# Out-projection products of the first token half moved from the sample sequences into the prompt attention, with the page gathers cut in two

## What is computed

```python
attn = nsa_attention(q, q_pos0, kv_cmp, kv_slc, kv_win, win_pos0, gates, w_cmp_k, w_cmp_v)
conv_out, conv_state = short_conv(xin, bg, cg, conv_prev, conv_w)
mix = jnp.einsum('bte,ed->btd', jnp.concatenate([attn, conv_out], axis=-1), w_out)
h = layer_norm(ALPHA * x + mix, ln1_g, ln1_b)
```

## Time and profile before

| | |
|---|---|
| Median of 3 runs | 2712.2 us |
| Profiled execution, its own time | 2708.6 us |
| Its span in the trace | 2706.8 us |
| PE busy | 2593.7 us, 96% |
| DVE, ACT, POOL busy | 74%, 40%, 3% |
| Granted TensorE clock, mean | 0.986 of full speed |
| DMA | 480.20 MB, 177 GB/s |
| Prompt attention | about 641 to 796 us |
| Sample sequences | about 796 to 1077 us |

### The profile page before, as it was taken

The page is one execution under the profiler, slowest core; times in us unless marked ns, Lnnn a source line. Parts: engine busy times, 40 slices in busy tenths (PEclk is TensorE's granted clock), DMA queues, the critical chain, the costliest instruction groups (busy, mean ns, idle before and its releaser), DMA issues.

```text
span 2706.8 us, 51737 instructions
## 1 busy us (share of the span) xinstructions
PE 2593.7 (96%) x20061; PEld 2477.8 (92%) x20061; DVE 2004.7 (74%) x3181; ACT 1073.2 (40%) x1361; POOL 70.3 (3%) x118
## 2 busy tenths in 40 slices
PE   8999999998889999987999999999999999999998
PEld 8999999995657777887999999999999999999997
DVE  5788732326875555689888888888888888888898
ACT  3111111115874444455555555555433333333333
POOL 1000000000000100000000000000000000000001
PEclk9999999998999999998999999999999999999998
DMA  8776643316026775754555555555795556555642
GB/s 260 231 240 207 191 85 79 79 49 237 2 71 213 246 247 176 213 158 138 187 185 187 190 189 188 185 185 185 277 313 181 185 177 211 184 182 180 194 126 86
DMA packets 514888, 480.20 MB, mean 177 GB/s; under 512 B 49276, under 2 KB 465300, under 8 KB 503862
## 3 DMA queue, kind: packets, MB, share of 16 engines
q1 hardware_dynamic: 509722, 411.57, 48.7%
q0 software_dynamic: 4736, 67.18, 6.6%
q10 hardware_dynamic: 332, 0.11, 0.0%
HBM read 387.89 MB, written 99.16 MB: 180 GB/s over the span
## 4 chain that ended last, share of the span: by engine, by line
PE 64%; DVE 6%; ACT 3%; issue 2%; DMA 1%; SPq 1%; DVEq 0%; ACTq 0%
PE ps L2619 50%; PE ps L2535 3%; PE ps L2462 3%; PE ps L2440 2%; PE ps L2330 1%; PE ps L2400 1%; PE ps L2384 1%; PE ps L2320 1%; DVE pS L1574 1%; PE ps L2344 1%; DMA f_b<-f_scratch 1%; PE ps L2416 1%; DVE w_sl L1774 0%; ACT sS L1000 0%; ACT pT L962 0%
## 5 line engine op out<-in xcount | busy, mean ns | idle before, releaser
L1128 ACT ACTIVATE w_sh<-w_s 128x1024 fp32r<-128x1024 f32 (+1 forms) x512 | 473.6, 949 | 783.3 <-PE ps L2619 522.6
L2619 PE MATMUL ps<-f_b,w_sh 128*128 128x288 f32 x3584 | 713.8, 295 | 8.4 <-DMA f_b<-f_scratch 6.0
L1774 DVE TENSOR_TENSOR w_sl<-w_s,w_sh 128x1024 fp32r<-128x1024 f32 (+1 forms) x512 | 554.3, 1088 | 123.9 <-ACT w_sh L1128 123.5
L2619 PEld LDWEIGHTS ps<-f_b,w_sh 128*128 128x128 f32 x3584 | 574.3, 189 | 11.0 <-DMA f_b<-f_scratch 7.0
L2619 PE MATMUL ps<-f_b,w_sl 128*128 128x288 f32 x1792 | 527.1, 294 | 0.0
L2619 PE MATMUL ps<-h_u,w_sh 128*128 128x288 f32 x2560 | 514.3, 296 | 11.4 <-DVE h_u L1909 10.9
L2619 PEld LDWEIGHTS ps<-h_u,w_sh 128*128 128x128 f32 x2560 | 411.1, 189 | 12.9 <-issue 6.8
L2619 PE MATMUL ps<-h_u,w_sl 128*128 128x288 f32 x1280 | 376.6, 294 | 0.0
L2619 PEld LDWEIGHTS ps<-f_b,w_sl 128*128 128x128 f32 x1792 | 338.9, 189 | 0.0
L861 ACT ACTIVATE w_hi<-w_raw 128x2048 fp32r<-128x2048 f32 x61 | 116.9, 1916 | 484.9 <-PE ps L2171 466.3
L2171 PE MATMUL ps<-x_hi,w_hi 128*128 128x288 f32 x1408 | 302.7, 297 | 0.0
(11 more groups left out here) (322 smaller groups left out, 3340.3 us busy)
## 6 DMA issues: line engine op xcount, KB each, us to landing
w_s<-in_w_mlp SPq DMA_DIRECT2D x512, 256.0 KB, 3.7
f_scratch<-f_st SPq DMA_DIRECT2D x32, 2016.0 KB, 9.0
f_b<-f_scratch SPq DMA_DIRECT2D x56, 1152.0 KB, 8.0
w_raw<-in_w_in SPq DMA_DIRECT2D x90, 512.0 KB, 5.1
e_raw<-in_w_out SPq DMA_DIRECT2D x16, 512.0 KB, 4.3
e_raw<-in_w_out SPq DMA_DIRECT2D x64, 128.0 KB, 3.3
wb<-in_cache_win SPq DMA_DIRECT2D x8, 1024.0 KB
w_raw<-in_w_out SPq DMA_DIRECT2D x64, 128.0 KB, 2.9
```

Of the source, the lines that this page charges most:

```text
L1128: nc.scalar.activation(w_sh[m][:, :, :], blocks, ACT.Copy).then_inc(z_h[m], 1)
L1774: nc.vector.tensor_tensor(w_sl[m][:, :, :], blocks, w_sh[m][:, :, :].bitcast(F32), ALU.subtract).then_inc(z_l[m], 1)
L2619: last = nc.tensor.matmul(ps[:, bank, 0:TH], w[b][:, at_, cols], acts(k, x), start=(start and n == 0), stop=(stop and n == 2), skip_group_ ...
```

## The change

- The convolution half of 13 of the 16 output tiles (CP = 13) becomes 26 steps of 12 products in the prompt attention: pair number j has step j - 3, for the pairs 3 to 28, between `p_pv` and the second `p_turn`. Their weights are loaded as 256 KB each into parts of `kvn` whose contents are stored by then. Each tile's sum goes by ACT (`c_copy`) and a store to scratch (`c_store`), and comes back as a third block of `e_xr`.
- The convolution half of the last three tiles is three whole steps in b = 0. The attention half of all 16 tiles is two steps in each of b = 1 to 7 and two behind. The second of the two is cut in halves, before and behind `k_qk(b, 3)`.
- Splitting the convolution part of `mix` moves into the first two pairs, `p_out` adds one tile per pair in place of four per eight units, in one PSUM bank rather than two (bank 7 goes to the new products).
- A gather of 2 MB becomes two of 1 MB with semaphores of their own, each issued when its own half of the buffer is free.
- `k_turn(b, 2)` comes before `s_turn(b - 1, 2)`; the copy of 8 MB becomes eight of 1 MB, between the loads of the first pairs.

```diff
-NE = 2 * KT
-E_FIRST = (0,) + tuple(2 + 4 * n for n in range(NB))
+CP = 13
+HS = 2 * CP
+ES = HS + KT - CP
+NE = ES + KT
+LAG = 3
...
+            sp.wait_ge(s_kvout, 16 * (3 * PT_TOK + 3))
             sp.wait_ge(s_xsave, 16 * 2 * KT // 4)
             e_load(0)
             e_load(1)
+            for e in range(2, HS):
+                e_load(e)
+                if e % 2 == 0 and e >= 4:
+                    c_store((e - 4) // 2)
+                if e < 2 + NB:
+                    sp.dma_start(kept[:, e - 2, :], rows_kept[:, e - 2, :]).then_inc(s_out, 16)
+            for n in range((HS - 4) // 2, CP):
+                c_store(n)
+            sp.wait_ge(s_pv, 2 + UNITS)
+            sp.wait_ge(s_of, UNITS // 2)
+            e_load(HS)
+            e_load(HS + 1)
+            sp.wait_ge(e_mm, HS)
             load_window(0)
+            e_load(HS + 2)
+            c_store(CP)
+            e_load(ES)
+            load_window(1)
+            c_store(CP + 1)
+            e_load(ES + 1)
+            c_store(CP + 2)
+            sp.wait_ge(e_tile, X_ROWS + 16 * KT)
             e_load_x(0)
-            e_load(2)
-            e_load(3)
-            load_window(1)
+            e_load_x(1)
             for b in range(1, NB):
-                e = E_FIRST[b]
-                e_load(e + 2)
-                e_store(e // 2 - 1)
-                e_load_x(e // 2)
-                e_load(e + 3)
-                e_load(e + 4)
-                e_store(e // 2)
-                e_load(e + 5)
-                e_load_x(e // 2 + 1)
+                n = 2 * (b - 1)
+                e_load(ES + n + 2)
+                e_store(n)
+                e_load(ES + n + 3)
+                e_load_x(n + 2)
...
             def seq_gather(m):
 
-                if m >= 3:
-                    pool.wait_ge(t_pv, 6 * ((m - 3) // 2) + 2 * ((m - 3) % 2) + 2)
-                nc.gpsimd.tensor_copy(idx1[m % 4][:, :], idx[:, m:m + 1]).then_inc(s_idx1, 1)
-                pool.wait_ge(s_idx1, 2 * NGATH + 2 * m + 1)
-                pool.sem_inc(s_idx1, 1)
-                nc.gpsimd.indirect_dma_start(
-                    sg[m % 3][:, :, :].rearrange("p j c -> p (j c)"), None, slc_rows,
-                    bass.IndirectOffsetOnAxis(ap=idx1[m % 4][:, 0:1], axis=0)).then_inc(s_sg[m % 3], 16)
+                for h in range(2):
+                    q = 2 * m + h
+                    if m >= 3:
+                        pool.wait_ge(t_pv, 6 * ((m - 3) // 2) + 2 * ((m - 3) % 2) + h + 1)
+                    nc.gpsimd.tensor_copy(idx1[q % 6][:, :], idx2[:, h, m:m + 1]).then_inc(s_idx1, 1)
+                    pool.wait_ge(s_idx1, 2 * NGATH + 2 * q + 1)
+                    pool.sem_inc(s_idx1, 1)
+                    nc.gpsimd.indirect_dma_start(
+                        sg[m % 3][:, 4 * h:4 * h + 4, :].rearrange("p j c -> p (j c)"), None, slc_rows,
+                        bass.IndirectOffsetOnAxis(ap=idx1[q % 6][:, 0:1], axis=0)).then_inc(s_sgh[h][m % 3], 16)
 
             seq_gather(0)
             seq_gather(1)
             pool.wait_ge(s_pv, 2 + UNITS)
-            pool.wait_ge(s_of, 2 + 2 * R)
+            pool.wait_ge(s_of, UNITS // 2)
...
+            def mix_high(j):
+
+                k, dst = (8, 12, 0, 4)[j], c_hi if j < 2 else m_hi
+                nc.scalar.activation(dst[:, k % 8:k % 8 + 4, :], mix[:, k:k + 4, 0:TH], ACT.Copy).then_inc(s_mhi, 1)
+
+            def e_split(e):
+
+                act.wait_ge(e_w[e % 2], e_in(e))
+                if e >= 2:
+                    act.wait_ge(e_mm, e - 1)
+                nc.scalar.activation(e_high(e), e_rawt(e), ACT.Copy).then_inc(e_his, 1)
+
+            def c_copy(n):
+
+                act.wait_ge(e_mm, c_step(n) + 1)
+                if n:
+                    act.wait_ge(e_tile, X_ROWS + 16 * n)
+                dst, src = c_place(n)
+                nc.scalar.activation(dst, src, ACT.Copy).then_inc(e_acc, 1)
+
+            def p_drain(u):
+
+                j = u // 2
+                if u % 2 and j > LAG and (j - LAG) % 2 and (j - LAG) // 2 < CP:
+                    c_copy((j - LAG) // 2)
+
+            def p_fill(u):
+
+                j = u // 2
+                if j == 0:
+                    mix_high(u)
+                if u % 2 and 1 <= j <= HS:
+                    e_split(j - 1)
+
             def p_act(r, last):
                 for u in range(16):
                     nk = UNIT_TILE[u % 8] + 1
                     act.wait_ge(s_pt_, u + 5 + 16 * r)
                     act.wait_ge(s_pv, max(u + 16 * r, 2))
                     nc.scalar.activation(pT[(u + 16 * r) % 3][:, 0:2 * nk, :].rearrange("p x q -> p (x q)"), flat(4, 2 * nk * P), ACT.Copy).then_inc(s_pe, 1)
+                    p_drain(u + 16 * r)
                     if u + 2 < 16 or not last:
...
+                x = e_xr[n % 2]
+                dve.wait_ge(e_mm, ES + n + 1)
+                dve.wait_ge(s_xr[n % 2], 32 * (n // 2 + 1))
+                nc.vector.scalar_tensor_tensor(x[:, 0, :], x[:, 0, :], ALPHA, ps[:, 2 + n % 2, 0:TH], ALU.mult, ALU.add).then_inc(e_acc, 1)
+                dve.wait_ge(e_acc, RES + 3 * n + 1)
+                nc.vector.scalar_tensor_tensor(x[:, 0, :], x[:, 1, :], ALPHA, x[:, 0, :], ALU.mult, ALU.add).then_inc(e_acc, 1)
+                dve.wait_ge(e_acc, RES + 3 * n + 2)
+                nc.vector.tensor_tensor(x[:, 0, :], x[:, 0, :], x[:, 2, :], ALU.add).then_inc(e_acc, 1)
+                dve.wait_ge(e_acc, RES + 3 * n + 3)
...
+            def p_out(j):
+                r, a, i = j // 8, j // 4 % 2, UNIT_TILE[2 * j % 8]
+                dve.wait_ge(s_pv, 2 + 2 * (j + 1))
+                tile = mix[:, 2 * r + a, i * P:(i + 1) * P]
+                nc.vector.tensor_tensor(tile, tile, ps[:, 6, i * P:(i + 1) * P], ALU.add).then_inc(s_of, 1)
...
+                    j = u // 2 + 8 * r
+                    if u % 2 and j < 2:
+                        mix_low(j)
+                    if u % 2 and j:
+                        p_out(j - 1)
+                    if u % 2 == 0 and 2 <= j < 2 + HS:
+                        e_low(j - 2)
...
-                if j % 4 == 0:
-                    pe.wait_ge(s_of, a + 1 + 2 * r)
+                if j + 8 * r:
+                    pe.wait_ge(s_of, j + 8 * r)
...
+            def e_part(e, j0, j1):
+
+                if e < HS:
+                    first, last_j, bank, start, stop = 4 * (e % 2), 4, 7, e % 2 == 0, e % 2 == 1
+                    n = e // 2
+                elif e < ES:
+                    n = e - HS + CP
+                    first, last_j, bank, start, stop = 0, 8, 2 + n % 2, True, True
+                else:
+                    n = e - ES
+                    first, last_j, bank, start, stop = 0, 8, 2 + n % 2, True, True
+                if j0 == 0:
...
+                    e = j + 8 * r - LAG
                     if j < 7 or not last:
                         p_qk(j + 1, r)
                     p_turn(2 * j, r)
                     if j or r:
                         p_pv((j - 1) % 8, r if j else r - 1)
+                    if 0 <= e < HS:
+                        e_part(e, 0, 4)
                     p_turn(2 * j + 1, r)
...
             k_turn(0, 0)
             k_turn(0, 1)
             k_qk(0, 0)
             k_turn(0, 2)
             k_qk(0, 1)
-            e_step(0)
+            e_step(HS)
             k_turn(0, 3)
             k_qk(0, 2)
+            e_step(HS + 1)
             k_turn(0, 4)
-            e_step(1)
             k_qk(0, 3)
+            e_step(HS + 2)
             k_qk(0, 4)
             k_qk(0, 5)
             for b in range(1, NB):
@@ -2492,20 +2607,19 @@
                 s_turn(b - 1, 1)
                 k_qk(b, 1)
                 s_pvs(b - 1, 0)
+                k_turn(b, 2)
                 s_turn(b - 1, 2)
                 s_pvs(b - 1, 1)
-                k_turn(b, 2)
-                e_step(e + 1)
                 k_qk(b, 2)
                 s_turn(b - 1, 3)
                 s_pvs(b - 1, 2)
                 s_turn(b - 1, 4)
                 s_pvs(b - 1, 3)
-                e_step(e + 2)
                 k_turn(b, 3)
-                e_step(e + 3)
+                e_part(e + 1, 0, 4)
                 k_qk(b, 3)
                 k_turn(b, 4)
+                e_part(e + 1, 4, 8)
                 s_turn(b - 1, 5)
                 s_pvs(b - 1, 4)
                 k_qk(b, 4)
@@ -2559,7 +2673,7 @@
```

More of the change, by code:

```diff
@@ L92 @@
 RAW_OUT_DMAS = 5
-NE = 2 * KT
-E_FIRST = (0,) + tuple(2 + 4 * n for n in range(NB))
+CP = 13
[3 more added lines that the diff above has]
+LAG = 3
+E_FIRST = (0,) + tuple(ES + 2 * n for n in range(NB - 1))
 FIRST_CHUNKS, CHUNKS = (0, 1, 2, 3, 4, 5), (0, 1, 4, 2, 3, 5)
@@ L308, in build @@
         idx = const("idx", [P, NGATH], U32)
-        idx1 = [const(f"idx1{i}", [P, 1], U32) for i in range(4)]
+        p_2 = const("p_2", [P, 2])
+        idx2 = const("idx2", [P, 2, NGATH], U32)
+        idx1 = [const(f"idx1{i}", [P, 1], U32) for i in range(6)]
         h_sum = const("h_sum", [P, T])
@@ L597, in _ @@
             load_x(1, 0)
```

(15 more changed lines are left out.)

227 lines of the change are left out of this document (121 added, 106 removed).

## The result

| | before | after |
|---|---|---|
| median of the runs (8 each, on one chip), us | 2711.4 | 2718.6 |
| lowest and highest | 2709.4, 2713.1 | 2714.7, 2721.6 |
| ratio, 95% interval | | 1.0029, 1.0019 to 1.0039 |
| span of the profiled execution | 2706.8 | 2716.3 |
| PE, DVE, ACT busy in it | | 2596.3, 2016.0, 1077.8 |

The change makes the kernel 0.29% slower (7.2 us between the medians), where 0.6% less was forecast. The forecast of 2697 and its range both miss.

A forecast was written before the change was run, and what follows sets the result against it. PE was taken to bound the sample loop, a three-engine chain the prompt attention. Prompt attention +27.5, b = 0 -2.5 and sample loop -40.3 sum to -15.3, from 2712.2 to 2697 us, range 2686 to 2713.

The forecast's parts named there:

- Step 1: Sample loop: PE waits 0.7 us for the first half gather in each of seven rounds, +4.9 us; none for the second.
- L: Sample loop: landing time of a 1 MB half gather after its issue, taken as 6.5 us, between 5.8 and 9.8.
- the path: Sample loop: time from the end of the first s_pvs to the fourth k_turn, put at 6.9 us.
- third rival: Sample loop: half gathers land no sooner than whole ones, 4.0 us wait at each fourth k_turn, 2720 us; chance 0.13.
- Step 2: Prompt attention: PE becomes the bound with no waits left, +4.0 us for each of six groups of four pairs.
- Rival 2: Prompt attention: none of the added work is hidden, +6.3 us a group, 2712 us, no change; chance 0.12.
- Step 3: Stage b = 0: a third step adds 3.2 us, but most waits for keys and window go, net -2.5 us.
- Step 4: Tail behind the sample loop, out-projection's second half and MLP: the same work, 0 us.
- Step 5: Start, ahead of the first p_qk: no difference, 0 us.
- Clock: Beginning of b = 1: the granted clock's dip to 0.54 costs about 1.5 us and may go; nothing counted.

The follow-up runs named there:

- early_load: The changed kernel with the sample loop's later attention weights loaded ahead of e_store(n) rather than behind it: 2713.4 us, ratio 1.0003 to before.
- whole_gather: The changed kernel with whole 2 MB gathers again, issued when both halves of the buffer are free: 2765.3 us, ratio 1.0201 to before.
- three_of_twelve: The changed kernel with nine of twelve products left out of each prompt step, waits and splits kept: 2712.6 us, ratio 0.9999 to before.
- small_splits: The changed kernel with the prompt steps' ACT and DVE splits cut to 64 of 512 columns, all products kept: 2716.9 us, ratio 1.0014.
- last_step: Changed kernel, attention weights and out-projection load issued earlier, twelve products before the fourth k_turn, b = 0's third step behind window scores: 2697.7 us, ratio 0.9944.
- tail_load: The changed kernel with the out-projection's first load issued ahead of the last round's e_store and e_load_x: 2715.0 us, ratio 1.0015 to before.
- swap: The changed kernel with twelve products of each round's second step ahead of the fourth k_turn, twelve ahead of its scores: 2715.1 us, ratio 1.0016.

## Why the prediction was wrong

**Step 1, the waits for the half gathers: +4.9.** They are 15.5. This is the largest term: it makes the sample loop miss by 9.8 of the 24.7 us by which the sum missed. The loop without its waits lost 46.0 us, where 45.2 were forecast, so the removal of two steps a round was priced rightly. Two sentences failed.

The first is "Wait: 6.5 + 1.1 - 6.9 = 0.7 us for each of seven". It was 1.6 a round, 11.3 in all: L was 7.0 on average rather than 6.5, up to 7.8, and the path 6.6 rather than 6.9. The second is "The other half is wanted 3.6 us later ... and issued 2.6 later: no further wait", which gives both halves one landing. The second half took 8.9 us, and the fifth turns waited 4.2 us for it.

Behind both stands what was said against the third rival, "nothing much else is in flight just then". I read that from the program before, whose `e_store` and loads had a longer round. The new SP order puts four transfers right there, and the round's four halves are issued within 7 us, where two whole gathers had 8.9 (903.81 and 912.7). early_load shows what the four transfers cost: 7.0 us of the waits, all of the fifth turns' 4.2 and 2.8 of the fourth's. With them gone L is 6.7, near the 6.5, and of the 8.5 us that are left, what goes beyond 4.9 is L's last 0.2 and the shorter path. The mean of a round (277 GB/s predicted, 255 measured) said nothing of a stretch at 380.

Rival 3 had the mechanism in part: transfers that interleave on the same engines. *The Trainium skill* (DMA: Bandwidth & Descriptors, Issuing engines are not separate DMA queues) states it, and early_load agrees with it: moving transfers of SP, no others, took 7 of the 15.5 us off POOL's gathers. Its size was wrong: L of 9.8 and 4.0 us at each fourth turn, 28 us in all, where L was at most 7.8 and all waits came to 15.5. That 2720 came out near is luck, as four other terms were short as well. Its claim that the half lands no sooner than the whole is refuted by whole_gather, where the whole takes 9.3 to 9.9 us at the same turn.

**Step 2, the group of the prompt: +4.0.** "PE becomes the bound and none of its waits is left" was nearly right: PE is busy for 22.6 of 23.3 us. Two sizes were off. Twelve products cost more than 1.58 us between their neighbours; that was half of the 3.17 of the earlier trace rows, and half of its other row, 3.38, is 1.69. PE's timeline of one step, its first and third product and the transposes behind the twelve:

```profile
697.82 0.40 PE L2477 MATMUL ps<-c_hi,kvn_r 128*128 128x288 f32 x1
...
698.19 0.30 PE L2477 MATMUL ps<-c_hi,g_lo 128*128 128x288 f32 x1
...
699.52 0.38 PE L2424 MATMUL ps<-ident,pS 128*128 128x128 f32 x2
```

That is 1.70 us from 697.82 to 699.52, as the first takes 0.24 until the next starts and the others 0.13. PE's busy time of a group came out at 22.6 rather than 22.4. And 0.7 us of idle time stayed. Together +4.9 a group; 0.9 more for each of six groups is 5.4 of the 5.6 that are missing. "ACT and DVE ... covered, with 2 to 4 us to spare": three_of_twelve keeps a group at 21.4 us, with PE waiting for DVE, which is busy for 17.7 to 19.0 in after's groups, so there were some 1.9 to spare; small_splits prices what leaks through at 0.7 a group. Rival 2 (nothing hidden) is refuted: +4.9, not +6.3.

**Step 3, b = 0: -2.5.** It was +0.8. The waits for the window's transfer did go. Those for ACT's copies of keys fell only from 4.1 us to 2.4, where most of them were to go. The third step waits 2.6 us for its own weights; I had it fill other waits, and did not walk its load. last_step takes that wait away.

**Step 4, the tail: nothing.** I priced SP's order nowhere past the loop. The load of the out-projection's first step moved behind a store and a load of x, ACT was held up by it, and PE by ACT: +3.1 by the trace, 3.6 by tail_load's time.

**Step 5, the start: nothing.** Right, as far as twelve traces of changed kernels show; the 2.9 us go with one execution's clock.

**Clock: nothing counted.** Right for after, where one dip remains (0.83 in 860 to 870, at b = 1, as before at 824). Wrong as a habit: in whole_gather, with waits of 6 to 7 us, the clock added half as much again.

By the rule of *the Trainium skill* that takes weight-load busy for the measure (Perfetto Trace Analysis, Identifying the Most-Contended Engine) the stage would have grown by nearly nothing. (The page calls matmul busy time no good measure of headroom; that it overstates is the prediction's reading.) It grew by 33.1, with weight loads busy 17.6 of 23.3 us and PE 22.6. Here PE's busy time was the better measure, as taken.

## What to carry to other kernels

When work leaves a loop that its bound engine fills, every transfer with a deadline in it must be walked anew against what else is issued in the same few microseconds, in the new program's queues; neither a mean rate nor a landing time of the old trace tells that, and transfers issued one behind the other don't all land after the same time (7.0 and 8.9 us here). If a wait remains, put independent work of the bound engine just ahead of it: the order of two pieces turned a tie (0.9996) into 0.29% faster. And filling an engine's holes in one stage is cheap only until the next engine's chain, its length rather than its busy time; find it by leaving the work out and looking at what the stage keeps.

## What the runs showed of the hardware

- In the sample loop a gather of 1 MB was there 6.4 to 7.8 us after its issue when it was the first of its round (after), one of 2 MB in the same place after 9.3 to 9.9 (whole_gather). The one issued 2.5 us behind it took 8.1 to 9.6 us, with four loads of 128 KB beside them and the engines at 360 to 380 GB/s, and no longer made PE wait when these loads were issued ahead. In swap's trace, which tells the landing of all 32 halves, they range thus:

```profile
DMA to landing us min/median/max: 6.2/9.2/11.8
```

- Waits of 6 to 7 us on PE, seven times, lowered the granted clock behind them (0.71 over 15 us, transposes at 1.94 us for 1.06), and so cost 1.5 times their length. Waits of 2.3 us left the clock at 1.00 in after's round.
- The same first 620 us of the changed kernels took 617.3 to 621.1 us, with a clock of 0.86 to 0.54 in the window 20 to 30, and their sample loops (whole_gather's aside) had none to five windows of 20 us with a dip. A single trace's account is good to some 3 us here, and so is the time of one run: after's eight lie within 7 us.
